# Output projection of the pooled groups two to four: seven block products for eight, added up in the PSUM banks

## The reference, cut to what matters

```python
def pool_mixer(h, w_in, w_group, scale, w_out):
    B, S, _ = h.shape
    u, z = jnp.split(h @ w_in, 2, axis=-1)
    p = causal_multiscale_pool(u).reshape(B, S, N_POOL_GROUPS, GROUP_WIDTH)
    y = jnp.einsum('bsgc,gcd->bsgd', p, w_group).reshape(B, S, A_WIDTH_2) * scale
    return (y * jax.nn.silu(z)) @ w_out
...
        x = x + gate[:, None, :] * y
```

## Time and profile before

| | |
|---|---|
| median of 3 runs | 2355.61 us (2354.32 to 2355.93) |
| the profiled execution, its span | 2354.7 us |
| PE busy | 2328.3 us (99% of the span), 11617 matmuls |
| DVE, ACT, POOL busy | 1535.8, 860.4, 1254.7 us |
| chain that ended last | PE 76%, DVE 6%, issue 4%, POOL 2% |
| granted TensorE clock, mean | 0.999 |

### The profile page before, as it was taken

How to read it: one execution, slowest core, us unless ns; L and a number is a source line. 1 busy time by engine, 2 the same in 40 slices (tenths; PEclk the granted TensorE clock), 3 DMA queues, 4 the chain that set the end, 5 groups by cost and what they waited for, 6 DMA issues and landing times.

```text
span 2354.7 us, 32347 instructions
## 1 busy us (share of the span) xinstructions
PE 2328.3 (99%) x11617; PEld 1943.6 (83%) x11617; DVE 1535.8 (65%) x1839; ACT 860.4 (37%) x1596; POOL 1254.7 (53%) x724
## 2 busy tenths in 40 slices
PE   9999999999999999999999999999999999999998
PEld 7888789888888888888888888778878788889887
DVE  7825556524578678788777777874572967147885
ACT  5212555612543222222222443122231244157773
POOL 4533955144145666766777434573654733467743
PEclk9999999999999999999999999999999999999999
DMA  5511011031011333333331111112121122210033
GB/s 220 157 45 46 19 19 37 1 116 45 19 42 50 117 124 117 125 125 117 123 124 64 63 45 45 58 53 78 54 76 67 58 67 109 79 37 24 24 115 137
DMA packets 67340, 178.85 MB, mean 76 GB/s; under 512 B 6994, under 2 KB 13908, under 8 KB 65120
## 3 DMA queue, kind: packets, MB, share of 16 engines
q1 hardware_dynamic: 57760, 147.80, 19.0%
q10 hardware_dynamic: 9104, 27.51, 3.4%
q0 software_dynamic: 368, 2.10, 0.5%
HBM read 161.61 MB, written 15.77 MB: 75 GB/s over the span
## 4 chain that ended last, share of the span: by engine, by line
PE 76%; DVE 6%; issue 4%; POOL 2%; ACT 1%; DMA 0%; POOLq 0%; DVEq 0%; ACTq 0%; SPq 0%
PE ps L704 21%; PE ps L705 20%; PE ps L707 20%; PE ps L854 4%; PE ps L832 3%; PE ps L842 2%; DVE trail L3532 1%; POOL split_lo L1653 1%; PE ps L2404 1%; PE ps L2420 1%; PE ps L2419 1%; PE ps L2389 1%; PE ps L2390 1%; ACT p L955 1%; PE ps L508 0%
## 5 line engine op out<-in xcount | busy, mean ns | idle before, releaser
L704 PE MATMUL ps<-h_hi,split_hi 128*128 128x512 f32 x1546 | 606.4, 392 | 3.7 <-DVE h_lo L3214 1.3
L705 PE MATMUL ps<-h_lo,split_hi 128*128 128x512 f32 x1546 | 601.1, 389 | 0.0
L707 PE MATMUL ps<-h_hi,split_lo 128*128 128x512 f32 x1546 | 536.2, 389 | 0.0
L1511 POOL TENSOR_TENSOR split_hi<-raw,cf 128x1024 fp32r<-128x1024 f32 x64 | 125.4, 1959 | 427.8 <-PE ps L707 373.4
L704 PEld LDWEIGHTS ps<-h_hi,split_hi 128*128 128x128 f32 x1546 | 290.7, 188 | 64.5 <-issue 2.5
L707 PEld LDWEIGHTS ps<-h_hi,split_lo 128*128 128x128 f32 x1546 | 290.8, 188 | 61.3
L705 PEld LDWEIGHTS ps<-h_lo,split_hi 128*128 128x128 f32 x1546 | 290.8, 188 | 56.4 <-issue 0.2
L1600 POOL TENSOR_TENSOR split_lo<-raw,split_hi 128x512 fp32r<-128x512 f32 x144 | 230.4, 1619 | 196.5 <-ACT split_hi L2717 196.3
L1653 POOL TENSOR_TENSOR split_lo<-raw,split_hi 128x512 fp32r<-128x512 f32 x84 | 128.1, 1534 | 179.5 <-ACT split_hi L2878 179.5
L2717 ACT CAST split_hi<-raw 128x512 fp32r<-128x512 f32 x144 | 87.0, 622 | 281.6 <-PE ps L707 205.4
L1513 POOL TENSOR_TENSOR split_lo<-raw,split_hi 128x1024 fp32r<-128x1024 f32 x64 | 178.4, 2787 | 5.0
(11 more groups left out here) (508 smaller groups left out, 5223.2 us busy)
## 6 DMA issues: line engine op xcount, KB each, us to landing
raw<-in_strips SPq DMA_DIRECT2D x208, 256.0 KB, 2.8
raw<-in_strips SPq DMA_DIRECT2D x86, 512.0 KB, 3.4
ada_raw<-in_ada SPq DMA_DIRECT2D x64, 512.0 KB, 3.6
memw_raw<-in_mem_strips SPq DMA_DIRECT2D x8, 512.0 KB, 5.8
xT<-in_xT ACTq DMA_DIRECT2D x4, 1024.0 KB, 7.9
x_spill_d<-xT ACTq DMA_DIRECT2D x1, 3584.0 KB, 10.1
xT<-x_spill_d ACTq DMA_DIRECT2D x2, 1792.0 KB, 9.3
out_T<-out_sb SPq DMA_DIRECT2D x13, 256.0 KB, 2.2
```

Of the source, the lines that this page charges most:

```text
L704: pe.matmul(acc[:, a:b], w_hi, hi[:, a:b], start=first, stop=False)
L705: pe.matmul(acc[:, a:b], w_hi, lo[:, a:b], start=False, stop=False)
L707: mm = pe.matmul(acc[:, a:b], w_lo, hi[:, a:b], start=False, stop=last)
L1511: pool.tensor_tensor(hi, raw[:, r, :], ones[:, 0:1].to_broadcast([P, D]), ALU.mult).then_inc(hi_split, 1)
```

## The change

**Output projection.** In groups two to four the 8 output tiles are made in two quads of 4 tiles (512 outputs), each by seven forms of 12 matmuls (forms 32 to 38 and 39 to 45), where it was four forms of 24. A form is split in two parts of 6 matmuls, one for each of two output tiles. The seven results are not combined in SBUF: PE goes on adding into a bank (`start=i in (0, 1, 3)`) while DVE adds the bank's content so far to one half of an `xT` tile after each part (`out_sum`, 28 for a group, 128x512, where `residual` had 8 of 128x1024). POOL makes four weight combinations for a quad, as in the other quads.

**Token combinations.** The gated tiles 0 and 1 hold in their second token half the difference of the halves (`first_difference`). Six half tiles (three combinations m = 2, 3, 4 of two tiles, "neg") are made by DVE, cast high by ACT, subtracted low by DVE. They lie in the second token half of `h_hi` and `h_lo`, tiles 0 to 5, whose content is written to DRAM at the start of group two (`h_keep_d`, two DMAs of 1.5 MB from ACT's queue) and brought back by POOL's queue after each of groups two and three (`keep_again`: four DMAs of 512 KB ahead of the next group's form 0, two ahead of its third weight combination). In the last group they lie in `pool_sums` and nothing is brought back.

**Order and places.** A group has 46 forms instead of 40; forms 44 and 45 use the places of 42 and 43. The loops over the groups on PE and POOL are written out. In the last group `xT` tiles become final in the order 4, 6, then 5, 7; the key/value strip starts with six tiles in place of five, squares come in the order of `KV_ORDER`, one square after each of forms 42 to 45 on ACT; the first strip's high part is cast by ACT where POOL did it.

```diff
-GROUP_FORMS = 40
+GROUP_FORMS = 46
+GROUP_SLOT = [p % 4 for p in range(42)] + [2, 3, 2, 3]
+OUT_BANKS = (((4, 6), (5, 7), (0, 1)), ((0, 2), (1, 3), (4, 5)))
+OUT_BANK = [0, 1, 0, 2, 0, 1, 0]
+OUT_AFTER = {2: 0, 4: 2, 5: 1, 6: 4}
+KV_ORDER = [0, 2, 1, 3, 4, 6, 5, 7]
...
+            def out_forms(g, quad):
+
+                j, at = 10 + 2 * quad, out_form(quad, 0)
+                group_half(pool, g, j, 0)
+                group_low(g, at, OUT_SOURCE[0])
...
+                pool.tensor_tensor(pool_form, a21, a22, ALU.add).then_inc(form_sum, 1)
+                group_low(g, at + 1, OUT_SOURCE[1])
+                summed(g, 4 + quad, 1)
+                pool.tensor_tensor(a21, a21, a11, ALU.subtract).then_inc(form_sum, 1)
...
+            def keep_again(g, m, done):
+                for low, of in enumerate((h_hi, h_lo)):
+                    at = slice(NEG_T[m], NEG_T[m] + 2)
+                    pool.dma_start(of[:, at, HALF:T], h_keep_d[low, :, at, :].bitcast(F32R)).then_inc(done, 16)
...
+                    if q == 0 and g > 1:
+                        group_through(pool, g - 1, out_form(1, 6))
+                        keep_again(g, 4, late_again)
...
+                if g < POOL_GROUPS - 1:
+                    group_through(pool, g, out_form(1, 4))
+                    keep_again(g, 2, h_again)
+                    keep_again(g, 3, h_again)
...
+            def out_quad(g, quad):
+
+                for i in range(7):
+                    p = out_form(quad, i)
+                    group_split(pe, g, p)
+                    if quad == 0:
+                        if i in (2, 4, 6):
+                            neg_lower(pe, g, i)
+                        else:
+                            gate_lower(pe, g, {0: 1, 1: 4, 3: 5, 5: 6}[i])
...
+                        elif i in OUT_AFTER:
+                            out_read(pe, g, 14 * quad + 2 * OUT_AFTER[i] + part + 1)
...
-            with pe.Fori(1, POOL_GROUPS) as g:
+            for g in range(1, POOL_GROUPS):
                 pool_group(g)
...
-            strip_part(S_KV, pair(2), range(5), before=as_split(pe, sp_kv))
-            pe.wait_ge(pool_res, 8 * POOL_GROUPS)
+            product(pe, pair(2), S_KV % 2, h_pieces(KV_ORDER[:6]), before=as_split(pe, sp_kv), stop=False)
+            out_read(pe, POOL_GROUPS - 1, 28)
             norm_sum(pe, n_kv)
...
+                if g == 1:
+                    sums_made(act, 1, 12)
+                    for low, of in enumerate((h_hi, h_lo)):
+                        act.dma_start(h_keep_d[low], rows(of[:, 0:6, HALF:T])).then_inc(h_kept, 16)
...
+                    if g == POOL_GROUPS - 1 and p >= GROUP_FORMS - 4:
+                        key_square(p - (GROUP_FORMS - 4))
...
+            def gates_low(g, n, out, src, hi):
+                gate_high(dve, g, n)
+                dve.tensor_tensor(out, src, rows(hi), ALU.subtract).then_inc(pool_ylo, 1)
...
+            def out_tokens_made(g):
+
+                first_difference(g, 0)
+                first_difference(g, 1)
+                gates_low(g, 3, y_lo[:, 0:2, t1], gates[:, 0:2, t1], y_hi[:, 0:2, t1])
+                gate_step(g, 2).then_inc(pool_g, 1)
...
+                neg_two(g, 0)
+                neg_three(g, 0)
+                difference_low(g, 0)
+                neg_four(g, 0)
+                neg_low(g, 2, 0)
+                gate_step(g, 3, t2).then_inc(pool_g, 1)
+                gate_made(dve, g, 4)
+                neg_two(g, 1)
+                neg_three(g, 1)
+                difference_low(g, 1)
+                gate_step(g, 3, t1).then_inc(pool_g, 1)
+                gate_made(dve, g, 5)
+                neg_four(g, 1)
+                neg_low(g, 2, 1)
+                out_sum(g, 0, 0, 0)
+                out_sum(g, 0, 0, 1)
+                gates_low(g, 4, y_lo[:, 2, :], gated_tile(2), gated_hi_tile(2))
...
+                        if g == POOL_GROUPS - 1 and quad and i < 4:
+                            key_low(i)
```

283 lines of the change are left out of this document (214 added, 69 removed).

## The result

The changed kernel takes **2403.4 us** (median of 4 runs, 2401.7 to 2403.6), the kernel before 2355.8 (2354.3 to 2356.1): a ratio of 1.0203 with a 95% interval of 1.0191 to 1.0215, 48 us slower. Forecast were 2366.3 us in a range to 2376.0. The direction was right and the size was missed by 37 us, more than three times the forecast loss.

The account below looks back on a forecast made before the run. PE, busy 99% of 2354.7 us, was taken to bound the kernel. Terms -16.3 + 0.5 + 15.3 + 4.6 + 4.2 + 2.1 + 0.3 gave +10.7 us, so 2366.3 us, in a range of 2356.5 to 2376.0.

Parts of the forecast that it names:

- Term 1: Output stages of groups two to four: 72 fewer matmuls at 0.2267 us each save 16.3 us; slower last-group forms add 0.5.
- Term 2: Form 33 in three groups: PE waits for the fourth pool_ylo behind ten DVE operations, 5.1 us each, +15.3.
- the low end: Form 33's wait in each group at its least, everything overlapped: 4.4 us, where 5.1 was taken.
- The rule that I weighed and set aside: Form 33: DVE operations with two SBUF inputs and POOL block each other; the three waits would cost +18.0, not +15.3.
- The bound of 6: Form 33's wait in each group at its most, 6 us, with one POOL split slowing DVE's lower half to 1.87.
- Term 3: Between groups, twice: POOL's DMA issues delay forms 0 and 3 by 0.2 and 2.1 us, together +4.6.
- Term 4: Last group's form 45 waits for DVE's sums behind ACT's late cast and square: +4.2, from 2.5 to 5.6.
- Term 5: Key/value norm after form 45: DVE's remaining work stalls PE 2.5 us in all, +2.1 net, bounds 0 and 4.5.
- Term 6: Start of group two: the 3 MB store delays some three of SP's loads by 1 to 2 us, +0.3, bounds 0 and 1.5.
- The clock: Rival, chance 0.23: PE's stalls of 4 to 5 us lower its clock, 2.3 us per return; four times 2375.5.
- stalls at full clock: The forecast's main case, chance 0.55: PE waits at the forecast places without its clock falling, 2366.3 us.
- the saving wins: Rival, chance 0.08: DVE and POOL keep pace, form 33 does not wait, gaps between groups halve, 2348.7 us.

## Why the prediction went wrong

**Term 1, the matmuls removed:** right. 11617 became 11545.

**Term 2, form 33 (5.1 each):** right in place and mechanism, short in size. The waits were 7.1, 7.1 and 7.4. The step that failed is "I stay near the low end since one POOL split stands in the stretch, not five". In group two's timeline three POOL operations meet DVE's SBUF-only ones. The one ahead of the fourth gate product made a token combination 0.9 us longer, and the gate product starts at 1622.39, 0.5 us after it could have. The one behind it costs 1.1, and the one beside the full-width lower half 0.5 (1.75 instead of 1.2). The chain of ten took 8.9 us instead of 7.4: with the late start, the 2.0 us by which 7.1 exceeds 5.1. The two versions that kept a POOL operation away from such a DVE operation show the cause: 1.60 became 0.69, and 3.31 became 1.21. The rule that I weighed and set aside had it nearer, though its 6.0 was short too. The bound of 6 was worked out for one split only.

**Term 3, between groups (2.3 each):** the place and the releaser were right, the price was not: 6.7 and 6.5. The step that failed is "the trace has POOL issues at 0.505 to 0.525 us, one behind the other". Two issues in a row say nothing about the fourth, which started only when all before it had landed (4.1 to 5.7 us of standing), and an issue of this shape takes 0.73 us. With the limit avoided, the rest of the term came out: 0.85 and 2.6 us where 0.2 and 2.1 stood.

**Term 4, form 45 (4.2):** 5.5, inside its bounds; the first key/value split beside DVE's addition is the 2.1 us by which it lies above the 3.4 of the run without that collision.

**Term 5, the norm (2.1 net):** 2.6, less the 0.4 of before. Right.

**Term 6, the store (0.3):** 3.6. The step that failed is "some three loads are late by 1 to 2 us and those have about 2 in hand". Four loads landed late, by 3.1 to 4.5 us, and at the start of the stage, where ACT casts a load as soon as it lands, nothing is in hand.

**The clock:** given as a rival with 0.23, and true. I forecast the main case "stalls at full clock", although the rows said that it falls within 5 us of idleness and my own terms made four stalls of 4 to 5 us. Its price of 2.3 us for each return was right: 2.1 to 2.5 behind each of the six long waits, 16.6 in all with the shorter ones. Its number, 2375.5, was built on my short waits and on four falls; the granted clock fell eight times in this stretch. The Trainium skill (TensorE: Matmul & The Clock Gate, HAM oscillation), which I had cited, says that waits of a few us send the engine back to its slow level and that the price is paid each time; the trace agrees. It deserved the forecast, not the rival. And "always at full clock so far" was misread. In the kernel before the clock falls once in the middle, behind the 16 short matmuls of an earlier norm sum, with 0.07 us of idle time ahead of them (the second row gives the busy times of a stretch, then the granted clock, 0.52):

```profile
1358.97 1.92 PE L508 MATMUL ps<-cf,sq_sum 128*128 128x1 f32 x16
1361.50:1365.00 3.50, 3.50 (x10) 2.70 (x9) 0.00 (x0) 0.00 (x0) 0.00 (x0) 0.52 0.00 0
```

About eight matmuls are slow there, 1.6 us. So part of what stands as slow behind the key/value norm sum may belong to that sum and not to its wait.

Of the 37 us missed the clock is 16.6, the gaps between groups 8.6, form 33 6.2, the store 3.3, form 45 1.3, and a split in group three 1.2 above its like before. All these errors have one sign. The terms that missed were set from rows taken with idle time around them, which the rival "the saving wins" had doubted in the other direction.
